# Expert layer, second phase: three dense sums kept in PSUM, dense steps spread over all units, route operations woven between the V rows

## What is computed

```python
def peer(h, lp):
    ...
    s1, i1 = lax.top_k(s[:, :, 0], PEER_TOPK)
    s2, i2 = lax.top_k(s[:, :, 1], PEER_TOPK)
    cand = (s1[..., :, None] + s2[..., None, :]).reshape(M, PEER_HEADS, PEER_TOPK * PEER_TOPK)
    cidx = (i1[..., :, None] * PEER_NKEYS + i2[..., None, :]).reshape(M, PEER_HEADS, PEER_TOPK * PEER_TOPK)
    top, j = lax.top_k(cand, PEER_TOPK)
    idx = jnp.take_along_axis(cidx, j, axis=-1).reshape(M, PEER_HEADS * PEER_TOPK)
    wts = jax.nn.softmax(top, axis=-1).reshape(M, PEER_HEADS * PEER_TOPK)
    ...
        u = jnp.take(pu, ii, axis=0)
        act = jax.nn.gelu(jnp.einsum('md,mkd->mk', xx, u), approximate=False)
        vv = jnp.take(pv, ii, axis=0)
        return jnp.einsum('mk,mkd->md', (act * ww).astype(xx.dtype), vv)
```

## Time and profile before

| | |
|---|---|
| median of 3 runs | 5562.33 us (5560.19 to 5563.29) |
| profiled execution | 5564.91 us, span 5563.0 us |
| expert stage | from about 3500 us to the end |
| VectorE, TensorE, GpSimd busy over the span | 60%, 82%, 26% |

### The profile page before, as it was taken

The page is one execution under the profiler, slowest core; times in us unless marked ns, Lnnn a source line. Parts: engine busy times, 40 slices in busy tenths (PEclk is TensorE's granted clock), DMA queues, the critical chain, the costliest instruction groups (busy, mean ns, idle before and its releaser), DMA issues. The chain is left out here.

```text
span 5563.0 us, 81870 instructions
## 1 busy us (share of the span) xinstructions
PE 4561.8 (82%) x30972; PEld 3114.4 (56%) x30972; DVE 3346.5 (60%) x7116; ACT 1297.9 (23%) x2733; POOL 1459.4 (26%) x1284
## 2 busy tenths in 40 slices
PE   7999997775777878799676674899999999999980
PEld 1899996554666667564576663344343434434430
DVE  0422332335555555112575552699999999999998
ACT  2100001332333333115155555010110111011001
POOL 0000000000111111000000000557566666656666
PEclk9999998667889888899878885999999999999995
DMA  5222223111000100412202203899999999999998
GB/s 217 87 93 92 92 92 110 56 64 60 28 23 24 34 27 11 174 69 77 105 15 78 69 24 109 347 374 385 353 383 358 380 361 369 385 350 382 360 353 299
DMA packets 354376, 1010.89 MB, mean 182 GB/s; under 512 B 39630, under 2 KB 120462, under 8 KB 349554
## 3 DMA queue, kind: packets, MB, share of 16 engines
q0 software_dynamic: 156672, 570.49, 26.3%
q1 hardware_dynamic: 197372, 435.99, 22.0%
HBM read 902.36 MB, written 103.99 MB: 181 GB/s over the span
## 5 line engine op out<-in xcount | busy, mean ns | idle before, releaser
L2509 PE MATMUL peer_v_b<-peer_vt,peer_mix 128*128 128x512 f32 x2048 | 944.4, 616 | 127.0 <-DVE peer_mix L2346 80.6
L2276 POOL DMA_INDIRECT peer_ring<-in_peer_u,peer_idx x544 | 596.4, 1096 | 1692.5 <-DVE peer_idx L2383 1266.6
L2497 PE MATMUL peer_s_b<-dense_hT_d,peer_ut 128*128 128x512 f32 x2048 | 901.3, 593 | 51.3 <-DMA peer_G2s<-mod 51.3
L2282 POOL DMA_INDIRECT peer_ring<-in_peer_v,peer_idx x544 | 715.4, 1315 | 293.0 <-issue 160.3
L2509 PEld LDWEIGHTS peer_v_b<-peer_vt,peer_mix 128*128 128x128 f32 x2048 | 402.5, 198 | 652.9 <-issue 498.5
L2497 PEld LDWEIGHTS peer_s_b<-dense_hT_d,peer_ut 128*128 128x128 f32 x2048 | 389.8, 190 | 542.2 <-issue 490.6
L2398 DVE SCALAR_TENSOR_TENSOR peer_acc<-peer_ring,peer_coef,peer_acc 128x1024 f32<-128x1024 f32 x534 | 653.9, 1280 | 0.0
L2435 DVE CUSTOM_DVE_ANT_0 peer_ring<-peer_ring,peer_h 128x1024 f32<-128x1024 f32 x544 | 637.5, 1220 | 2.0 <-DVE peer_h L2412 1.0
L1357 POOL TENSOR_TENSOR rw_An<-rw_abT,rw_join 128x256 f32<-128x256 f32 x160 | 126.0, 794 | 1924.8 <-DVE rw_abT L1267 1542.5
L56 PE MATMUL proj_acc<-proj_hT_high,proj_w_low 128*128 128x352 f32 x1584 | 512.2, 323 | 25.8 <-DVEq L353 25.8
L57 PE MATMUL proj_acc<-proj_hT_low,proj_w_high 128*128 128x352 f32 x1584 | 508.6, 321 | 0.0
(11 more groups left out here) (418 smaller groups left out, 7015.3 us busy)
## 6 DMA issues: line engine op xcount, KB each, us to landing
peer_ut<-in_peer_ut SPq DMA_DIRECT2D x128, 512.0 KB, 9.9
peer_vt<-in_peer_v SPq DMA_DIRECT2D x128, 512.0 KB, 7.9
pT<-proj_o SPq DMA_DIRECT2D x66, 528.0 KB, 3.0
proj_w<-in_w_in SPq DMA_DIRECT2D x66, 512.0 KB, 4.2
G<-route_G SPq DMA_DIRECT2D x16, 2048.0 KB, 16.6
peer_gt<-G SPq DMA_DIRECT2D x128, 256.0 KB, 5.9
mod_w<-in_w_ada SPq DMA_DIRECT2D x12, 2048.0 KB, 8.2
peer_ring<-in_peer_u,peer_idx POOLq DMA_INDIRECT x544, 10.2
```

What stands on the lines that cost most here:

```text
L2276: pool.indirect_dma_start(out=ring[:, k, :], out_offset=None, in_=t["peer_u"], in_offset=bass.IndirectOffsetOnAxis(ap=idx[U % 2][:, k:k + ...
L2282: pool.indirect_dma_start(out=ring[:, k, :], out_offset=None, in_=t["peer_v"], in_offset=bass.IndirectOffsetOnAxis(ap=idx[U % 2][:, k:k + ...
L2497: last = pe.matmul(s_b[:, n % 3, :], ut[:, n % UT, k, :], hT_d[:, k, :], start=(k == 0), stop=(k == KD - 1))
L2509: last = pe.matmul(v_b[:, m % 4, :], mix[:, part % 2, e, tokens], vt[:, part % 2, e, cols], start=(e == 0), stop=(e == PART - 1))
```

## The change

Three of the eight dense outputs (0, 1, 2) get PSUM banks of their own (`kept_b`) in which they are summed over all 32 parts, and are copied out once at the end. The other five take turns in three banks; the score banks become two. The dense steps become one list of mixes and adds, spread over nine places in each of the 34 units (five among the dots, four among the V rows), except for the last six. The route becomes a generator of small steps: four run behind the dots, then two behind each V row. Its one-hot products are made for both lists in one instruction. ScalarE's gelu for the next tile stands at the place of a tile's mix. The dense output moves from unit 32 to the end of the kernel. The first phase keeps the old router as `OldRouter`.

```diff
+    def mark(self, ins):
+        self.n += 1
+        ins.then_inc(self.sem, 1)
+        return self.n
+    def need(self, n):
+        self.eng.wait_ge(self.sem, self.base + n)
...
+KEPT, TURNING = 3, 3
+TURNS = ((3, 0), (4, 1), (5, 2), (6, 7))
+ORDER = [o for outs in TURNS for o in outs]
+TURNING_ORDER = [o for o in ORDER if o >= KEPT]
+EARLY, EXP_AT = 4, 9
...
+    def after(self, dve, ch, n):
+        if n is not None:
+            ch.need(n)
+        dve.sem_inc(self.passed, 1)
+    def top16(self, dve, ch, n, vals, val, place):
+        for half in range(2):
+            o8 = slice(8 * half, 8 * half + 8)
+            self.after(dve, ch, n)
+            n = ch.mark(dve.max(val[:, o8], vals))
+            yield n
+            self.after(dve, ch, n)
+            n = ch.mark(dve.max_index(place[:, o8], val[:, o8], vals))
+            yield n
+            if half == 0:
+                self.after(dve, ch, n)
+                n = ch.mark(dve.match_replace(vals, val[:, o8], vals, LOWEST))
+                yield n
...
+    def pairs(self, dve, ch, c, best_ready):
+        top, pos = self.top[:, c % 2, :, :], self.pos[:, c % 2, :, :]
+        dve.tensor_copy(self.posf[:, :, :], pos)
...
+        for n in self.top16(dve, ch, n, self.cand[:, :, :].rearrange("p a b -> p (a b)"), self.best, self.j16):
+            yield
+        ch.need(n)
+        dve.tensor_scalar(self.z[:, 1:2], self.best[:, 0:1], -1.0, None, ALU.mult).then_inc(best_ready, 1)
...
-        s_b, v_b = s.ps("s_b", [P, 3, 512]), s.ps("v_b", [P, 4, 512])
+        s_b, v_b, kept_b = s.ps("s_b", [P, 2, 512]), s.ps("v_b", [P, TURNING, 512]), s.ps("kept_b", [P, KEPT, 512])
...
+        dense = []
+        for part in range(UNITS):
+            for e, outs in enumerate(TURNS):
+                if part + 1 < UNITS:
+                    dense.append(("mix", PART * (part + 1) + e))
+                dense += [("add", (part, o)) for o in outs if o >= KEPT]
+        places = [("dots", k) for k in (2, 5, 8, 11, 15)] + [("v", k) for k in (1, 5, 9, 13)]
+        steps_at, done = {}, 0
+        for n, (U, place) in enumerate((U, place) for U in range(ALL) for place in places):
+            upto = min(-(-(n + 1) * len(dense) // (len(places) * ALL - 6)), len(dense))
+            steps_at[U, place] = dense[done:upto]
+            done = upto
...
                 for U in range(ALL):
-                    ahead = [n for n in range(PART * (U + 1), PART * (U + 2)) if n < EXPERT_TILES]
-                    for n in ahead[0:2]:
-                        gelus(n)
+                    for k in range(TOP):
+                        if ("dots", k) in places:
+                            ahead(U, ("dots", k))
                     act.wait_ge(dots_ready, U + 1)
                     act.activation(act_d[:, :], dots[:, :], ACT.Gelu).then_inc(gelu_ready, 1)
...
-                    if U + 1 < UNITS:
-                        route_keys(route_at["unit", U + 1])
+                    stream = iter(())
+                    if U + 1 < UNITS:
+                        stream = route(route_at["unit", U + 1], idx[1 - U % 2][:, :], idx_ready)
...
+                    for _ in range(EARLY):
+                        next(stream, None)
                     dve.wait_ge(gelu_ready, U + 1)
...
                     ch.link(dve.tensor_tensor(coef[:, :], act_d[:, :], weights, ALU.mult))
-                    if U + 1 < UNITS:
-                        route_pairs(idx[1 - U % 2][:, :], idx_ready)
...
                     for k in range(TOP):
                         add_v(U, k)
-                        if k in (2, 6, 9, 12):
-                            next(steps, None)
+                        for _ in range(2):
+                            next(stream, None)
+                        dense_steps(U, ("v", k))
...
+                dve.wait_ge(o_summed, OUTS * UNITS)
+                for o in range(KEPT):
+                    dve.tensor_copy(acc_d[:, o // 2, (o % 2) * 512:(o % 2 + 1) * 512], kept_b[:, o, :]).then_inc(kept_read, 1)
                 total(ALL - 1)
...
-                    if n >= 3:
-                        pe.wait_ge(gelued, n - 2)
+                    if n >= 2:
+                        pe.wait_ge(gelued, n - 1)
...
+                    if o < KEPT:
+                        bank, first, last_part = kept_b[:, o, :], part == 0, part == UNITS - 1
+                    else:
+                        n = added(part, o)
+                        bank = v_b[:, (n - 1) % TURNING, :]
+                        if n > TURNING:
+                            pe.wait_ge(o_added, n - TURNING)
...
+                for part in range(UNITS):
+                    for e, outs in enumerate(TURNS):
+                        if part + 1 < UNITS:
+                            scores(PART * (part + 1) + e)
+                        for o in outs:
+                            sums(part, o)
```

More of the change, by code:

```diff
@@ L1847, in peer_routes, with weave @@
+def weave(*streams):
+    streams = list(streams)
+    while streams:
+        for x in list(streams):
+            if next(x, streams) is streams:
+                streams.remove(x)
 def peer_routes(nc, t, hT_d):
@@ L2193, in peer_experts, with added @@
         route_at = {route: c for c, route in enumerate(routes)}
+        dense = []
[10 more added lines that the diff above has]
+            done = upto
+        assert done == len(dense)
+        def added(part, o):
+            return part * (OUTS - KEPT) + TURNING_ORDER.index(o) + 1
         with nc.Block() as block:
@@ L2293, in gelus @@
                         act.wait_ge(mixed, n - 1)
-                    act.activation(gelu[:, n % 2, :], s_b[:, n % 3, :], ACT.Gelu).then_inc(gelued, 1)
+                    act.activation(gelu[:, n % 2, :], s_b[:, n % 2, :], ACT.Gelu).then_inc(gelued, 1)
                 def exps(c):
@@ L2324, in _ @@
                         finish(U // HEADS, P)
[L2325 to L2331, removed]
+                act.wait_ge(kept_read, KEPT)
+                act.wait_ge(o_added, (OUTS - KEPT) * UNITS)
+                trash = mix[:, 0, 0:2, :].rearrange("p a c -> p (a c)")
+                for i in range(DENSE):
+                    ch.link(act.activation(trash, acc_d[:, i, :], ACT.Square, accum_out=ss[:, 1 + i:2 + i]))
+                ch.link(act.activation(ss[:, 1:], ss[:, 1:], ACT.Ln, bias=eps[:, :], scale=1.0 / D))
+                act.activation(ss[:, 1:], ss[:, 1:], ACT.Exp, scale=-0.5).then_inc(msd_ready, 1)
                 finish(TILES_G, NS)
@@ L2347, in mixes, with adds, dense_steps @@
                                       ALU.mult).then_inc(mixed, 1)
-                def adds(m):
-                    part, o = divmod(m, OUTS)
+                def adds(part, o):
                     to = acc_d[:, o // 2, (o % 2) * 512:(o % 2 + 1) * 512]
-                    dve.wait_ge(o_summed, m + 1)
+                    n = added(part, o)
+                    dve.wait_ge(o_summed, OUTS * part + ORDER.index(o) + 1)
                     if part:
-                        dve.wait_ge(o_added, m - OUTS + 1)
-                        dve.tensor_tensor(to, to, v_b[:, m % 4, :], ALU.add).then_inc(o_added, 1)
-                    else:
[L2357 to L2363, removed]
-                            mixes(n)
[L2365 to L2369, removed]
+                        dve.wait_ge(o_added, n - (OUTS - KEPT))
+                        dve.tensor_tensor(to, to, v_b[:, (n - 1) % TURNING, :], ALU.add).then_inc(o_added, 1)
+                    else:
+                        dve.tensor_copy(to, v_b[:, (n - 1) % TURNING, :]).then_inc(o_added, 1)
+                def dense_steps(U, place):
+                    for kind, n in steps_at.get((U, place), ()):
+                        if kind == "mix":
+                            mixes(n)
+                        else:
+                            adds(*n)
                 def samples_head(head):
@@ L2373, in samples_head, with route @@
                     return idx_all[:, cols], w_all[:, cols]
-                def route_keys(c):
+                def route(c, to, ready):
                     dve.wait_ge(sc_in[c % SC], 16 * (c // SC + 1))
[L2377 to L2383, removed]
+                    yield from r_.keys(dve, ch, c, sc[:, c % SC, :, :], keys_done)
+                    yield from r_.pairs(dve, ch, c, best_ready)
+                    dve.scalar_tensor_tensor(out=to, in0=r_.sel[:, 0, :], scalar=float(KEYS), in1=r_.sel[:, 1, :],
                                              op0=ALU.mult, op1=ALU.add).then_inc(ready, 1)
@@ L2422, in deal @@
                     dve.wait_ge(dealt, 2 * GROUPS)
-                route_keys(0)
-                route_pairs(idx[0][:, :], idx_ready)
+                weave(route(0, idx[0][:, :], idx_ready))
                 route_weights(0, w[0][:, :])
@@ L2485, in _ @@
                 ch.link(dve.tensor_copy(acc[0:NS, 0, :].rearrange("p (g c) -> p g c", g=2), v_b[0:NS, 0:2, :]))
+                dve.wait_ge(msd_ready, 1)
```

(6 more changed lines are left out.)

128 lines of the change are left out of this document (79 added, 49 removed).

## The result

The changed kernel takes 5599.13 us (median of 5 runs, 5575.90 to 5616.25) beside 5560.19 us for the kernel before (5 runs, 5550.68 to 5563.29): a ratio of 1.0073, 95% interval 1.0042 to 1.0104. It is slower, where 5525 us was forecast. The profiled execution took 5616.25 us, the longest of the five, with a span of 5614.4 us: 51.4 us over the profiled span before.

The account below looks back on a forecast made before the run. VectorE's instruction stream was taken to bound the expert stage. From 5563 us, dense adds -64, route -65, tail +15, late index +70 and smaller waits +6 gave 5525 us; whole range 5462 to 5590, the forecast's own 5480 to 5570.

Parts of the forecast that it names:

- Dense adds, -64: VectorE, units 0 to 31: 8 adds a part become 5, so 107 fewer steps of 0.6 us, -64 us.
- route operations, -65: VectorE's next route, mostly paired behind V rows: fewer waits between linked operations save 2.1 us for 31 routes, -65 us.
- Late index, +70: Units following a plain one: U gathers start some 8 us ahead, not 20; dots stall 3.5 us in 20 units, +70 us.
- three bounds for the stall: Landing of U row 15: 2.3 us late by GpSimd alone, 3.8 by bytes, 10.6 at unit 10's spacing.
- the slide: Dense steps shift against the units, 8.52 a unit where a part has 9.
- the burst: SP's dense loads, claimed to meet the U gathers in some units only; stall taken as 3.5 us.
- the late index costs more than the instructions saved: Rival: first dots of plain units wait for U rows, 6.5 us stall, 5585 us; chance 0.17.
- the null at 5.4 us a unit: Stall of plain units at which the late index cancels the savings: (5563 - 5455) / 20 = 5.4 us.
- the first rival: Nothing is given back: plain units fall to 52.5 us and transfers keep up, 5455 us with small waits; chance 0.20.
- Tail, +15: Kernel's end: the dense output, free in unit 32 before, now stands behind the last fold, +15 us, bounds 11 and 17.
- Smaller waits, +6: VectorE waiting for late score loads and for the activation behind ScalarE's gelu: together +6 us, bounds 0 and 30.
- TensorE's pace through ScalarE: Rival: the score group is late at a third of the 34 activations, +77 us, 5602 us; chance 0.06.

Follow-up runs that it names:

- Run 1: The changed kernel with the whole route behind the dots again, so the index is early, dense part as changed: 5527.5 us, 0.9939 of the kernel before.
- run 3: The changed kernel with four route operations behind each V row, not two: 5538.12 us, 0.9969 of the kernel before.
- run 7: The changed kernel with route operations between the dots, gelu at its own mix, score loads ahead of dense loads: 5410.77 us, 0.9752 of the kernel before.

## Why the prediction was wrong

The direction was wrong because one term was mis-sized; the mechanism and its place were as written. Two of the signs that the prediction names for being wrong came: plain units of over 58 us (8 of the 12 that follow a plain one and hold no sample route themselves) and, in unit 0, coefficients that wait for the activation.

- **Dense adds, -64, and route operations, -65: right.** Undisturbed plain units are 52.7 us (52.5 worked out). Run 1 against the kernel before and against the kernel after splits this into 1.7 and 2.2 us a unit (2.0 and 2.1). Over the nine units without a stall (7, 8, 11, 15, 16, 19, 23, 24, 27) the two together are 4.0 us, 4.2 worked out; unit 3, without a stall too, is only 2.3 us shorter, and why stays open. (The prediction's V row of 1.22 us is the dot's time in the earlier trace rows; a V row is 1.28 there, and no sum changes by it.)
- **Late index, +70: the step that failed.** The index came 8.9 us ahead, as worked out, and the units that stall are those named. But the stall is 6.5 us a plain unit, 130 us in 20 units. GpSimd's part was as worked out: 15 gathers at 1.60 us are the 24 us of the sum, though 2.29 us is the slowest gather among the dots and not the pace there, which is 1.68 us (1.76 taken). What was wrong is the last landing, 10.1 us after its issue (mean of the 20 units) where the sum has 5.8. Of three bounds for the stall (2.3, 3.8 and 10.6 us) I took 3.5, near the one with half a unit's dense loads. I wrote that the slide makes the burst meet the gathers "in some units only", and then gave it no weight of its own: it met them in 8 of 20, at 9.8 us each, while the other 12 had 4.3. The rival "the late index costs more than the instructions saved" had just this, half at 10.6 and half at 2.3, 6.5 us and 5585 us. The bound by bytes also took the full 419 GB/s from the first landing on; in unit 13 the rate was 320 for the first 18 us (last section). The rival got 0.17; the null at 5.4 us a unit, which it names, lay between the two bounds that I had worked out from rows, and nothing in the rows put the mean under it with the 0.75 that the forecast and the first rival held together.
- **Tail, +15: right**, 12.2 us, within its bounds of 11 and 17.
- **Smaller waits, +6: too small.** ScalarE's gelu of the next tile stands ahead of the activation of the dots, and in unit 0 that gelu waits for TensorE. The coefficients of the kernel after then wait 11.5 us there:

```profile
3580.43 0.60 ACT L2426 ACTIVATE peer_gelu<-peer_s_b 128x512 f32<-128x512 f32 x1 [13.14 <-PE peer_s_b L2625]
...
3580.92 0.21 ACT L2453 ACTIVATE peer_act_d<-peer_dots 128x16 f32<-128x16 f32 x1
...
3581.16 0.18 DVE L2582 TENSOR_TENSOR peer_coef<-peer_act_d,peer_w 128x16 f32<-128x16 f32 x1 [11.49 <-ACT peer_act_d L2453]
```

  I had looked at plain units, where TensorE is ahead; in unit 0 it has just begun. Unit 0 is 15.7 us longer, within the bounds of 0 to 30. The wait for scores in units 28 to 30 exists (run 1) but is hidden by the stalls in the kernel after.
- **TensorE's pace through ScalarE** did not show: past unit 0 the coefficients wait 2.5 us in all. But the stalls hid some of it: in run 3, where they go, the same wait is 18.8 us past unit 0 (30.3 less 11.5), so ScalarE's new order is not hidden by TensorE's 2 us a unit alone, as the prediction took it to be.

The sum with the measured terms: stage units 1 to 31, -4.0 x 30 units + 0.5 for unit 31 + 130 + 6.8 for V rows that now wait for landings gives +17, where the trace has 18.2; with unit 0, the tail and units 32 and 33 that is +44, and the other 6.4 us stand ahead of the change's stage.

## What to carry to other kernels

Before an instruction that releases transfers is moved behind other work to save its engine a few instructions, work out its lead, and size what is lost at the busiest meeting of transfers that the new schedule allows, not at a mean: where the cost has two levels, give each level its count. An operation chain is better hidden ahead of the release than behind it: between the dots it cost no lead at all, and each operation alone between two rows saved nearly its whole link (0.20 us to the next instruction, not 0.43). And when a step is put ahead of another in an engine's order, look at the first unit too, where the producers have no lead yet.

## What the runs showed of the hardware that I had not expected

A gather's time from issue to landing isn't its own: the median over the plain stretch of stage was 7.5 us in the kernel after (3738 to 5447 us) and 13.6 us in run 7 (3700 to 5240 us), which is the faster by far, since its gathers are issued 20 us ahead.

```profile
peer_ring<-in_peer_u,peer_idx POOLq DMA_INDIRECT x448, 7.5
```

```profile
peer_ring<-in_peer_u,peer_idx POOLq DMA_INDIRECT x448, 13.6
```

And while the late gathers of unit 13 were on their way, the DMA engines were not full at first: 320 GB/s in the first 18 us, 404 in the next 15 (windows of the kernel after, columns as above).

```profile
4338.00:4356.00 18.00, 12.38 (x23) 5.10 (x23) 16.50 (x28) 0.60 (x1) 14.95 (x11) 0.81 0.89 320
4356.00:4371.00 15.00, 10.22 (x19) 4.14 (x18) 7.16 (x12) 0.60 (x1) 11.78 (x11) 0.77 1.02 404
```

So the dots wait for transfers in a unit whose DMA share is only 0.93, where the units of run 7, at 1.03, wait for none: the lead decides, not the mean rate.
